# Streaming both parts of x in one 512-column matmul for the feature-form products of a two-layer block in fp32r

## The chip, the cores and the metric

One Trainium2 chip, one of its cores. The metric is the device time of one execution in microseconds. Engines: TensorE (PE) does matmuls, ScalarE (ACT) and VectorE (DVE) elementwise work, GpSimd (POOL) small steps, SyncE (SP) starts the DMAs.

## What is computed

Two transformer-like layers over 256 tokens of width 1024, in float32. Layer one: an mLSTM branch, a gated short convolution and a stick-breaking attention, all fed by one projection of the normalised input, merged by sigmoid gates; then a squared-ReLU MLP:

```python
h = rmsnorm(x, norm_mix_g)
proj = h @ w_in                        # 1024 x 15368, split in 15 parts
merged = (sigmoid(g_ml) * (y_ml @ w_ml_proj) + sigmoid(g_sc) * (y_sc @ w_sc_proj)
          + sigmoid(g_sb) * (y_sb @ w_sb_proj))
x = x + merged @ w_out
h2 = rmsnorm(x, norm_mlp_g)
x = x + square(relu(h2 @ w_up)) @ w_down       # 1024 x 4096, 4096 x 1024
```

Layer two mixes an RG-LRU branch, gated linear attention and block attention from `w_in_2`, projects with `w_out_2`, and has a gated feed-forward part of width 2816 (`w_ffn_gate_2`, `w_ffn_up_2`, `w_ffn_down_2`).

## The kernel before

All weights stream once through SBUF. A product is made of groups of up to 512 output columns; a group's weights come in units of 4 k-tiles (4 x 128 rows) by 512 columns, 1 MB each. `land` has three slots for units; SP loads unit u once `wlo` of unit u-3 is made.

Each float32 operand is split in two fp32r parts. For weights, `split(u)` does it: ACT copies `land` to `whi` (line 865), DVE subtracts to get `wlo` (line 1210); both have three slots, and ACT waits until PE has done unit u-3. For activations the parts are `xT_hi` and `xT_lo` and the like, made when a transposed tile leaves PSUM (`turn_split`). A product is hi x hi + hi x lo + lo x hi: three matmuls.

In `product(u, between)` token-form groups hold 128 tokens stationary and stream up to 512 weight columns (lines 500 to 502). Feature-form groups hold 128 weight columns stationary and stream the 256 tokens of x three times: `whi` against `xT_hi`, `whi` against `xT_lo`, `wlo` against `xT_hi` (lines 508, 510, 512), all into the same 256 columns of PSUM. `acc` has two halves of two banks each, taken by groups in turn: group n waits until group n-2 has been read.

Feature-form are the queries and keys of both attentions, the short convolution's parts (scc, scu, scb), up0 to up7, and in layer two lru, mqk0, mqk1, gqk and gu0 to gu10, a gate and an up part of 256 columns each in one group. The rest is token-form.

The order on each engine is written out by hand. The loops of ACT and DVE run over units u. At u each first does `split(u + 2)`, then the steps listed for that u, among them the eviction if u is the last unit of its group. ACT and DVE work in order, so whatever waits there holds all that stands behind it:

- up: DVE waits for PE, does max(acc, 0) x row from PSUM (line 1669), ACT squares it (1134) and rounds it to `aT_hi` (1137); DVE makes `aT_lo` (1469) in the next iteration, after its `split`.
- gu: DVE multiplies the gate part (1741) and the up part (1743) by the row, ACT takes the sigmoid (1186), DVE multiplies twice (1747, 1748), ACT rounds to `a2T_hi` (1188), DVE makes `a2T_lo` (1476) an iteration later.
- scb: DVE multiplies `conv` (1624), ACT rounds (1128), DVE subtracts (1628); `conv_taps` is twelve small steps (1307, 1309).

Between products PE also does the attention heads and the turns (transposes, line 527). Before up, lru and gu the input is normalised anew: `turn_split` of h2, h3, h4, squares on ACT, a root on POOL, a diagonal on DVE (1225) and a `row`.

Of the kernel before, what the change touches and what calls it, by code (L numbers as in the profile page):

```python
# [5 lines left out]
F32 = mybir.dt.float32  # L6
# [5 lines left out]
P = 128  # L12
# [59 lines left out]

def plan_groups():

    g = []

    def halves(name, weight, col, act, form, k=KD):
        for j in range(2):  # L80
            g.append((f"{name}{j}", weight, [(col + j * NG, NG)], k, act, form))

    halves("sbq", "w_in", C_SBQ, "xT", "feat")
    halves("sbk", "w_in", C_SBK, "xT", "feat")
    halves("sbv", "w_in", C_SBV, "xT", "tok")
    halves("mlq", "w_in", C_MLQ, "xT", "feat")
    halves("mlk", "w_in", C_MLK, "xT", "feat")
    halves("mlv", "w_in", C_MLV, "xT", "tok")
    halves("mlo", "w_in", C_MLO, "xT", "tok")
    halves("scc", "w_in", C_SCC, "xT", "feat")  # L90
    halves("scu", "w_in", C_SCU, "xT", "feat")
    halves("scb", "w_in", C_SCB, "xT", "feat")
    for b, col in (("sb", C_GSB), ("ml", C_GML), ("sc", C_GSC)):
        for j in range(2):
            g.append((f"g{b}{j}", "w_in", [(col + j * NG, NG)], KD, "xT", "tok"))
            g.append((f"p{b}{j}", f"w_{b}_proj", [(j * NG, NG)], KD, f"y{b}T", "tok"))
    halves("out", "w_out", 0, "mT", "tok")
    for j in range(D_FF // NG):
        g.append((f"up{j}", "w_up", [(j * NG, NG)], KD, "xT", "feat"))
# [5 lines left out]
    g.append(("gqk", w2, [(C2_GQ, 2 * P)], KD, "xT", "feat"))
    g.append(("gout", w2, [(C2_GOUT, GLA_H * GLA_DV)], KD, "xT", "tok"))
    g.append(("mv", w2, [(C2_MV, NG)], KD, "xT", "tok"))
    g.append(("mqk1", w2, [(C2_MQ + 2 * P, 2 * P), (C2_MK + 2 * P, 2 * P)], KD, "xT", "feat"))
    halves("mix", "w_out_2", 0, "y2T", "tok")
    for j in range(D_FF2 // GU):  # L110
        g.append((f"gu{j}", ("w_ffn_gate_2", "w_ffn_up_2"), [(j * GU, GU), (j * GU, GU)], KD, "xT", "feat"))
    halves("dn", "w_ffn_down_2", 0, "a2T", "tok", KF2)
    return g


GROUPS = plan_groups()
G_AT = {grp[0]: n for n, grp in enumerate(GROUPS)}
UNITS = [(n, k, min(UK, grp[3] - k)) for n, grp in enumerate(GROUPS) for k in range(0, grp[3], UK)]


_at = UNITS.index((G_AT["mix0"], 0, UK))
UNITS[_at:_at + 4] = [(G_AT[f"mix{j}"], k, m) for k, m in ((0, 4), (4, 2), (6, 2)) for j in range(2)]
# [7 lines left out]
def width(n):  # L130
    return sum(w for _, w in GROUPS[n][2])
# [20 lines left out]
for _name, _k, _ in TURNS:  # L152
# [7 lines left out]
U_IF = 1  # L160
TURN_SB = ML0 + 6
TURN_ML = TURN_SB + 2
B2 = FIRST_U["lru"]

MB_AT = [(B2 + 11, 4), (B2 + 12, 2), (B2 + 12, 4), (B2 + 13, 2), (B2 + 14, 1), (B2 + 14, 3), (B2 + 15, 1),
         (B2 + 15, 2), (B2 + 15, 4), (B2 + 16, 1), (B2 + 16, 2)]
MB_TURN0, MB_TURN1 = (B2 + 15, 3), (B2 + 17, 1)


def build(nc, dram, out):  # L170
# [19 lines left out]
    row = sb("row", [P, T])  # L190
    vecs = sb("vecs", [P, V_ROWS])
# [68 lines left out]
    relu = sb("relu", [P, 2, 2 * NG], stack=ffn)  # L260
    relu2 = sb("relu2", [P, 2, 2 * NG], stack=ffn)
# [55 lines left out]
    half_hi, half_lo = sem("half_hi"), sem("half_lo")  # L317
# [42 lines left out]
    def land_count(u):  # L360

        return 16 * sum(len(GROUPS[UNITS[v][0]][2]) for v in range(u % LANDS, u + 1, LANDS))
# [5 lines left out]
    def _(sp):  # L368
# [17 lines left out]

        for u in range(NU):
# [8 lines left out]
            if u == 5:  # L396
# [5 lines left out]
            if u == FIRST_U["up1"]:  # L402
# [3 lines left out]
            if u == B2 + 4:  # L406
# [29 lines left out]
    def _(pe):  # L436
# [12 lines left out]
        def wait_operand(name, act, k1):  # L449

            if act == "xT":
                turned_ready("h2" if name[:2] == "up" else
                             "h4" if name[:2] == "gu" else
# [7 lines left out]
            elif act == "yscT":  # L461
                pe.wait_ge(ysc_lo, (k1 + 3) // 4)
# [10 lines left out]
        def product(u, between):  # L473
# [12 lines left out]
            if u == 0:  # L486
                pe.wait_ge(half_lo, 1)
# [1405 lines left out]
```

## Time and profile before

| | us |
|---|---|
| median of 3 runs | 964.78 (964.78 to 964.8) |
| span of the profiled execution | 964.4 |
| PE busy | 935.6 (97%) |
| DVE busy | 579.0 (60%) |
| ACT busy | 469.0 (49%) |
| DMA, mean of 16 engines | 170 GB/s |
| mean granted TensorE clock | 0.991 |

The share of busy time counts when an engine has any instruction under way. For PE it includes overlap of one matmul with the next, so the spacing of starts tells more.

### The profile page before, as it was taken

The numbers are of one execution on the slowest core, as the hardware profiler recorded it, in microseconds if no ns is written. First come the engines' busy times: TensorE is split into PE (matmuls) and PEld (weight loads), VectorE is DVE, ScalarE is ACT, GpSimd is POOL, SyncE is SP. The second block draws the span as 40 slices with busy tenths as digits, with TensorE's granted clock in tenths as the row PEclk, the third lists the DMA queues.
The fourth block names the chain that finished last, engine by engine and source line by source line (L and its number), as shares of the span: only waits on it lengthen the run. The fifth ranks groups of instructions, "written<-read, shape, count | busy, mean of one in ns | idle before, by whom it ended". The sixth has DMA issues, their size and how long they took to land.

```text
span 964.4 us, 14152 instructions
## 1 busy us (share of the span) xinstructions
PE 935.6 (97%) x6003; PEld 842.0 (87%) x6003; DVE 579.0 (60%) x610; ACT 469.0 (49%) x520; POOL 38.6 (4%) x75
## 2 busy tenths in 40 slices
PE   5999999999999999999999999998999799999996
PEld 4998998899998888888999988898788699999884
DVE  4554645577787445555556644557975666666552
ACT  6334776862445334344555534446654554444341
POOL 0000111120010000000000000010000000000000
PEclk9999999999999999999999999999999799999999
DMA  8567444443255655555555565528612555556641
GB/s 265 186 234 230 147 161 144 133 150 113 88 175 178 207 184 199 193 175 196 175 175 175 175 218 177 195 77 259 218 67 69 171 176 176 175 176 200 211 135 44
DMA packets 99375, 164.01 MB, mean 170 GB/s; under 512 B 4833, under 2 KB 37316, under 8 KB 99185
## 3 DMA queue, kind: packets, MB, share of 16 engines
q1 hardware_dynamic: 99312, 163.11, 51.9%
q8 instruction: 47, 0.77, 0.3%
q14 instruction: 16, 0.12, 0.0%
HBM read 162.03 MB, written 3.16 MB: 171 GB/s over the span
## 4 chain that ended last, share of the span: by engine, by line
PE 93%; DVE 2%; DMA 2%; ACT 2%; issue 1%; SPq 1%; POOL 0%; DVEq 0%; ACTq 0%; POOLq 0%
PE acc L508 14%; PE acc L500 14%; PE acc L510 14%; PE acc L512 14%; PE acc L502 14%; PE acc L501 14%; DMA land<-in_w_in 2%; PE m L527 1%; PE m L574 1%; PE m L563 1%; PE m L552 1%; DVE wlo L1210 0%; ACT lw L988 0%; DVE x_tok L1486 0%; PE m L636 0%
## 5 line engine op out<-in xcount | busy, mean ns | idle before, releaser
L1210 DVE TENSOR_TENSOR wlo<-land,whi 128x2048 fp32r<-128x2048 f32 (+2 forms) x153 | 337.1, 2206 | 242.1 <-ACT whi L865 240.4
L865 ACT ACTIVATE whi<-land 128x2048 fp32r<-128x2048 f32 (+2 forms) x153 | 281.7, 1846 | 233.4 <-PE acc L502 164.5
L508 PE MATMUL acc<-xT_hi,whi 128*128 128x256 f32 x1168 | 335.3, 287 | 2.1 <-DVE xT_lo L1247 1.8
L510 PE MATMUL acc<-xT_lo,whi 128*128 128x256 f32 x1168 | 332.2, 284 | 0.0
L512 PE MATMUL acc<-xT_hi,wlo 128*128 128x256 f32 x1168 | 332.1, 284 | 0.0
L508 PEld LDWEIGHTS acc<-xT_hi,whi 128*128 128x128 f32 x1168 | 225.8, 193 | 6.8 <-issue 4.2
L510 PEld LDWEIGHTS acc<-xT_lo,whi 128*128 128x128 f32 x1168 | 225.9, 193 | 0.1
L512 PEld LDWEIGHTS acc<-xT_hi,wlo 128*128 128x128 f32 x1168 | 225.8, 193 | 0.0
L500 PE MATMUL acc<-whi,xT_hi 128*128 128x512 f32 (+2 forms) x240 | 91.9, 383 | 0.0
L502 PE MATMUL acc<-whi,xT_lo 128*128 128x512 f32 (+2 forms) x240 | 90.5, 377 | 0.0
L501 PE MATMUL acc<-wlo,xT_hi 128*128 128x512 f32 (+2 forms) x240 | 90.3, 376 | 0.0
L500 PEld LDWEIGHTS acc<-whi,xT_hi 128*128 128x128 f32 x240 | 45.4, 189 | 9.1 <-issue 0.7
L502 PEld LDWEIGHTS acc<-whi,xT_lo 128*128 128x128 f32 x240 | 45.3, 189 | 8.3
L501 PEld LDWEIGHTS acc<-wlo,xT_hi 128*128 128x128 f32 x240 | 45.4, 189 | 7.8
L500 PE MATMUL acc<-whi,aT_hi 128*128 128x512 f32 x128 | 50.6, 396 | 0.0
L501 PE MATMUL acc<-wlo,aT_hi 128*128 128x512 f32 x128 | 50.6, 395 | 0.0
L502 PE MATMUL acc<-whi,aT_lo 128*128 128x512 f32 x128 | 50.6, 395 | 0.0
L501 PE MATMUL acc<-wlo,a2T_hi 128*128 128x512 f32 x88 | 34.8, 395 | 0.0
L502 PE MATMUL acc<-whi,a2T_lo 128*128 128x512 f32 x88 | 34.8, 395 | 0.0
L500 PE MATMUL acc<-whi,a2T_hi 128*128 128x512 f32 x88 | 34.8, 395 | 0.0
L1186 ACT ACTIVATE sig<-act 128x512 f32<-128x512 f32 x11 | 7.0, 633 | 47.4 <-DVE act L1741 47.4
L502 PEld LDWEIGHTS acc<-whi,aT_lo 128*128 128x128 f32 x128 | 24.0, 187 | 5.9
(337 smaller groups left out, 1077.7 us busy)
## 6 DMA issues: line engine op xcount, KB each, us to landing
land<-in_w_in SPq DMA_DIRECT2D x56, 1024.0 KB, 5.1
land<-in_w_up SPq DMA_DIRECT2D x16, 1024.0 KB, 5.3
land<-in_w_down SPq DMA_DIRECT2D x16, 1024.0 KB, 5.1
land<-in_w_ffn_gate SPq DMA_DIRECT2D x22, 512.0 KB, 4.1
land<-in_w_ffn_up SPq DMA_DIRECT2D x22, 512.0 KB, 5.3
land<-in_w_ffn_down SPq DMA_DIRECT2D x10, 1024.0 KB, 5.2
land<-in_w_out SPq DMA_DIRECT2D x6, 1024.0 KB, 5.1
land<-in_w_in SPq DMA_DIRECT2D x12, 512.0 KB, 4.5
```

The lines of the kernel that those rows point to most:

```text
L500: mm(to, xh[:, k0 + k, ts], whi[:, s, k, 0:w], start=first, stop=False)
L501: mm(to, xh[:, k0 + k, ts], wlo[:, s, k, 0:w], start=False, stop=False)
L502: last = mm(to, xl[:, k0 + k, ts], whi[:, s, k, 0:w], start=False, stop=end)
L508: mm(to, whi[:, s, k, cs], xh[:, k0 + k, :], start=first and c % 2 == 0, stop=False, skip_group_check=True)
L510: mm(to, whi[:, s, k, cs], xl[:, k0 + k, :], start=False, stop=False, skip_group_check=True)
L512: last = mm(to, wlo[:, s, k, cs], xh[:, k0 + k, :], start=False, stop=end, skip_group_check=True)
L527: last = nc.tensor.transpose(M[bank + b][:, (i * TT + t) * P:(i * TT + t + 1) * P], src[:, t, col0 + k * P:col0 + (k + 1) * P], ident)
L552: mm(z[:, 0:T], sbkT[o:o + SB_D, c, 0:P], sbqT[o:o + SB_D, c, :], start=True, stop=True)
L563: mm(z[:, 0:3 * P], sums_r[:, 0:P], w, start=False, stop=True, skip_group_check=True)
L574: last = mm(to, a[:, at:at + P], sbv[:, t, v], start=False, stop=True, skip_group_check=True)
L865: activate(whi[:, u % PARTS, 0:m, 0:w], land[:, u % LANDS, 0:m, 0:w], ACT.Copy).then_inc(hi_ready, 1)
L1210: v.tensor_tensor(wlo[:, u % PARTS, 0:m, 0:w], land[:, u % LANDS, 0:m, 0:w], whi[:, u % PARTS, 0:m, 0:w].bitcast(F32), ALU.subtract).then_ ...
```

## The change

Feature-form products stream x's two parts in one matmul. `xT` now holds both parts side by side, `[P, KD, 2, T]`; `whi` against it gives 512 columns into one bank, hi x hi in the first half and hi x lo in the second; `wlo` against `xT_hi` adds 256 columns to the second half. A bank now holds 128 features, so a group has 256 (two banks) and not 512, and a unit of 2048 columns is 8 k-tiles by 256. The two halves are added at eviction: ACT copies the second half to `rest` (`rest_copy`), DVE adds it to the first (`join`). Constant scales move from the eviction into the weight split. sbq0 with sbq1, up0 with up1, lrx with lrg and ga0 with gu0 are woven in units of 4 k-tiles. The gated part has separate groups ga and gu. The scratch of software DMA is set to 8192.

```diff
-        for j in range(2):
-            g.append((f"{name}{j}", weight, [(col + j * NG, NG)], k, act, form))
+    def quarters(name, weight, col, n=4):
+        for j in range(n):
+            g.append((f"{name}{j}", weight, (col + j * FW, FW), KD, "xT", "feat"))
...
+        step = KD if form == "feat" and name not in PAIRED and name != "gqk" else UK
...
+PAIRED = ("sbq0", "sbq1", "up0", "up1", "lrx", "lrg", "ga0", "gu0")
...
                     for c in range(w // P):
-                        to = acc[:, n % 2, c // 2, (c % 2) * T:(c % 2 + 1) * T]
                         cs = slice(c * P, (c + 1) * P)
-                        mm(to, whi[:, s, k, cs], xh[:, k0 + k, :], start=first and c % 2 == 0, stop=False,
-                           skip_group_check=True)
-                        mm(to, whi[:, s, k, cs], xl[:, k0 + k, :], start=False, stop=False,
-                           skip_group_check=True)
-                        last = mm(to, wlo[:, s, k, cs], xh[:, k0 + k, :], start=False, stop=end,
+                        mm(acc[:, n % 2, c, :], wh[:, k, cs], xT[:, k0 + k].rearrange("p i t -> p (i t)"), start=first,
+                           stop=False, skip_group_check=True)
+                        last = mm(acc[:, n % 2, c, T:2 * T], wl[:, k, cs], xh[:, k0 + k, :], start=False, stop=end,
                                   skip_group_check=True)
...
+        def rest_copy(n):
+
+            at = FEATS.index(n)
+            product_done(GROUPS[n][0])
+            if at >= 2:
+                act.wait_ge(read_dve, reads_before(FEATS[at - 2], "dve"))
+            activate(rest[:, at % 2], rest_part(n), ACT.Copy).then_inc(rest_out, 1)
...
+            if ends and name[:3] == "scb" or ends and name[:2] == "up":
+                rest_copy(n)
...
+            if ends and GROUPS[n][5] == "feat" and name[:3] != "scb" and name[:2] != "up":
+                rest_copy(n)
...
+        def join(to, n):
+
+            dve.wait_ge(rest_out, FEATS.index(n) + 1)
+            return v.tensor_tensor(to, main_part(n), rest[:, FEATS.index(n) % 2], ALU.add)
...
-                v.scalar_tensor_tensor(out=relu[:, j % 2, :].rearrange("p (a b) -> p a b", b=T),
-                                       in0=flat.rearrange("p (a b) -> p a b", b=T), scalar=0.0,
-                                       in1=along(4), op0=ALU.max, op1=ALU.mult).then_inc(read_dve, 1)
+                r = relu[:, j % 2, :].rearrange("p (a b) -> p a b", b=T)
+                link(join(r, n))
+                v.scalar_tensor_tensor(out=r, in0=r, scalar=0.0, in1=along(2), op0=ALU.max,
+                                       op1=ALU.mult).then_inc(read_dve, 1)
...
+                a = act2[:, j % 2, :].rearrange("p (a b) -> p a b", b=T)
+                join(a, n).then_inc(read_dve, 1)
+                dve.wait_ge(read_dve, reads_before(n, "dve"))
+                v.tensor_tensor(a, a, along(2), ALU.mult).then_inc(gate2_ready, 1)
+            if ends and name[:2] == "gu":
+                j = int(name[2:])
+                product_done(name)
+                a, b = act2[:, j % 2, :], up2[:, j % 2, :].rearrange("p (a b) -> p a b", b=T)
+                link(join(b, n))
+                v.tensor_tensor(b, b, along(2), ALU.mult).then_inc(read_dve, 1)
```

ACT's steps for ga are `rest_copy`, a wait for `gate2_ready` and the sigmoid; for gu `rest_copy`, a wait for `act2_ready` and the copy to `a2T_hi`. For scb and up `rest_copy` stands right behind `split(u + 2)`, before ACT's wait for DVE. The steps of the second mixer are moved by two units.

## Rows read from the trace of the kernel before

**Rows 1.** The page: busy time of the engines, and the chain that ended last

```profile
PE 935.6 (97%) x6003; PEld 842.0 (87%) x6003; DVE 579.0 (60%) x610; ACT 469.0 (49%) x520; POOL 38.6 (4%) x75
...
PE 93%; DVE 2%; DMA 2%; ACT 2%; issue 1%; SPq 1%; POOL 0%; DVEq 0%; ACTq 0%; POOLq 0%
```

**Rows 2.** Timeline of PE (start, length in us): feature form, then token form

```profile
499.79 0.28 PE L508 MATMUL acc<-xT_hi,whi 128*128 128x256 f32 x1
...
502.91 0.28 PE L512 MATMUL acc<-xT_hi,wlo 128*128 128x256 f32 x1
...
199.78 0.39 PE L500 MATMUL acc<-whi,xT_hi 128*128 128x512 f32 x1
...
201.82 0.39 PE L500 MATMUL acc<-whi,xT_hi 128*128 128x512 f32 x1
```

**Rows 3.** Groups by line and shape: count, busy us, mean ns, idle before, releaser

```profile
L508 PE MATMUL acc<-xT_hi,whi 128*128 128x256 f32 x1168 | 335.3, 287 | 2.1 <-DVE xT_lo L1247 1.8 <-issue 0.3
...
L1210 DVE TENSOR_TENSOR wlo<-land,whi 128x2048 fp32r<-128x2048 f32 x141 | 322.4, 2289 | 229.7 <-ACT whi L865 229.5
L865 ACT ACTIVATE whi<-land 128x2048 fp32r<-128x2048 f32 x141 | 269.2, 1912 | 221.3 <-PE acc L502 156.1 <-PE acc L512 61.1 <-DMA land<-in_w_in 3.8
```

**Rows 4.** Timeline of ACT and DVE in the up stage

```profile
480.63 1.89 ACT L865 ACTIVATE whi<-land 128x2048 fp32r<-128x2048 f32 x1
...
482.56 2.29 DVE L1210 TENSOR_TENSOR wlo<-land,whi 128x2048 fp32r<-128x2048 f32 x1 [4.02 <-ACT whi L865]
484.77 1.22 DVE L1469 TENSOR_TENSOR aT_lo<-relu,aT_hi 128x1024 fp32r<-128x1024 f32 x1
...
488.83 1.23 DVE L1669 SCALAR_TENSOR_TENSOR relu<-acc,row 128x1024 f32<-128x1024 f32 x1 [0.65 <-PE acc L512]
```

**Rows 5.** Timeline of DVE and ACT at one group of the gated stage

```profile
803.27 0.69 DVE L1747 TENSOR_TENSOR act<-act,sig 128x512 f32<-128x512 f32 x1
803.99 0.69 DVE L1748 TENSOR_TENSOR act<-act,up 128x512 f32<-128x512 f32 x1
...
804.72 0.63 ACT L1188 ACTIVATE a2T_hi<-act 128x512 fp32r<-128x512 f32 x1 [1.49 <-DVE act L1748]
805.25 1.90 ACT L865 ACTIVATE whi<-land 128x2048 fp32r<-128x2048 f32 x1
```

**Rows 6.** Timeline of PE: first matmul of up0, of down0, of gu0 and dn0

```profile
452.78 0.28 PE L508 MATMUL acc<-xT_hi,whi 128*128 128x256 f32 x1
...
546.23 0.39 PE L500 MATMUL acc<-whi,aT_hi 128*128 128x512 f32 x1
...
763.04 0.55 PE L508 MATMUL acc<-xT_hi,whi 128*128 128x256 f32 x1 [1.14 <-DVE xT_lo L1247]
...
893.83 0.39 PE L500 MATMUL acc<-whi,a2T_hi 128*128 128x512 f32 x1
```

**Rows 7.** Timeline of DVE: first wlo after the diagonal of h2, h3 and h4

```profile
461.20 4.49 DVE L1210 TENSOR_TENSOR wlo<-land,whi 128x2048 fp32r<-128x2048 f32 x2 [0.32 <-ACT whi L865]
...
647.35 2.48 DVE L1210 TENSOR_TENSOR wlo<-land,whi 128x1088 fp32r<-128x1088 f32 x2
...
774.30 4.49 DVE L1210 TENSOR_TENSOR wlo<-land,whi 128x2048 fp32r<-128x2048 f32 x2 [0.33 <-ACT whi L865]
```

**Rows 8.** Timelines: DVE at the convolution's taps, ACT and PE under the heads

```profile
286.23 1.14 DVE L1307 TENSOR_SCALAR conv<-zT,vecs 128x256 f32<-128x256 f32 x4
287.41 3.38 DVE L1309 SCALAR_TENSOR_TENSOR conv<-zT,vecs,conv 128x256 f32<-128x256 f32 x8
...
115.34 1.90 ACT L865 ACTIVATE whi<-land 128x2048 fp32r<-128x2048 f32 x1
...
114.71 1.45 PE L574 MATMUL m<-sbv,sba 128*128 128x64 f32 x12
```

**Rows 9.** Timeline of PE, then PE busy, granted clock, DMA share, GB/s by stretch

```profile
690.38 1.91 PE L694 MATMUL m<-gv,kl_tok 64*128 64x256 f32 x6 [2.10 <-DVE kl_tok L1361]
...
692.00:694.00 2.00, 2.00 (x5) 0.50 1.05 350
```

More of the change, by code:

```diff
@@ L70, with halves @@
     V_ROWS += _rows
+FW = 2 * P
 def plan_groups():
     g = []
-    def halves(name, weight, col, act, form, k=KD):
+    def halves(name, weight, col, act, k=KD):
         for j in range(2):
-            g.append((f"{name}{j}", weight, [(col + j * NG, NG)], k, act, form))
[L83 to L87, printed above, removed]
@@ L93, in plan_groups @@
+    quarters("sbk", "w_in", C_SBK)
+    halves("sbv", "w_in", C_SBV, "xT")
+    quarters("mlq", "w_in", C_MLQ)
+    quarters("mlk", "w_in", C_MLK)
+    halves("mlv", "w_in", C_MLV, "xT")
+    halves("mlo", "w_in", C_MLO, "xT")
+    quarters("scc", "w_in", C_SCC)
+    quarters("scu", "w_in", C_SCU)
+    quarters("scb", "w_in", C_SCB)
     for b, col in (("sb", C_GSB), ("ml", C_GML), ("sc", C_GSC)):
         for j in range(2):
-            g.append((f"g{b}{j}", "w_in", [(col + j * NG, NG)], KD, "xT", "tok"))
@@ L105, in plan_groups @@
[L105 to L112, printed above, removed]
+            g.append((f"g{b}{j}", "w_in", (col + j * NG, NG), KD, "xT", "tok"))
@@ L113, in plan_groups, with plan_units, weave @@
+    halves("dn", "w_ffn_down_2", 0, "a2T", KF2)
     return g
 GROUPS = plan_groups()
+FEATS = [n for n, grp in enumerate(GROUPS) if grp[5] == "feat"]
 G_AT = {grp[0]: n for n, grp in enumerate(GROUPS)}
-UNITS = [(n, k, min(UK, grp[3] - k)) for n, grp in enumerate(GROUPS) for k in range(0, grp[3], UK)]
-_at = UNITS.index((G_AT["mix0"], 0, UK))
-UNITS[_at:_at + 4] = [(G_AT[f"mix{j}"], k, m) for k, m in ((0, 4), (4, 2), (6, 2)) for j in range(2)]
+def plan_units():
+    u = []
+    for n, (name, _, _, k, _, form) in enumerate(GROUPS):
+        step = KD if form == "feat" and name not in PAIRED and name != "gqk" else UK
+        u += [(n, at, min(step, k - at)) for at in range(0, k, step)]
+    def weave(first, pieces):
+        at = u.index((G_AT[first], 0, UK))
+        u[at:at + 4] = [(G_AT[first] + j, k, m) for k, m in pieces for j in range(2)]
+    for first in PAIRED[::2]:
+        weave(first, ((0, 4), (4, 4)))
+    weave("mix0", ((0, 4), (4, 2), (6, 2)))
+    return u
@@ L130, in width @@
 def width(n):
-    return sum(w for _, w in GROUPS[n][2])
+    return GROUPS[n][2][1]
+SCALED = {"sbq": SB_D ** -0.5, "mlk": ML_D ** -0.5, "mq0": MB_D ** -0.5, "mq1": MB_D ** -0.5}
 def readers(name):
@@ L360, in land_count, with piece, main_part, rest_part @@
     def land_count(u):
-        return 16 * sum(len(GROUPS[UNITS[v][0]][2]) for v in range(u % LANDS, u + 1, LANDS))
+        return 16 * (u // LANDS + 1)
+    def piece(of, slot, u):
+        n, _, m = UNITS[u]
+        return of[:, slot, 0:m * width(n)].rearrange("p (k n) -> p k n", n=width(n))
+    def main_part(n):
+        return acc[:, n % 2, :, 0:T]
+    def rest_part(n):
+        return acc[:, n % 2, :, T:2 * T]
     block = ctx.enter_context(nc.Block())
@@ L401, in _ @@
                 sp.dma_start(by_query, by_distance.to_broadcast([P, MB_H * 2 * T])).then_inc(copies_out, 16)
-            if u == FIRST_U["up1"]:
+            if u == FIRST_U["up2"]:
                 sp.wait_ge(turn_lo, TURN_AT["merged"] + 4)
@@ L1182, in _ @@
                 act.wait_ge(read_act, reads_before(n, "act"))
-            if ends and name[:2] == "gu":
+            if ends and name[:2] == "ga":
                 j = int(name[2:])
@@ L1732, in _ @@
                 residual(6)
-            if ends and name[:2] == "gu":
+            if ends and name[:2] == "ga":
                 j = int(name[2:])
```

299 lines of the change are left out of this document (146 added, 153 removed).

## The prediction

> **What bounds the kernel now.** I read the page's busy line and its chain that ended last first: TensorE is busy for 97% of the span, and 93% of the chain is PE, spread over the six matmul lines of `product` [rows 1]. Such a busy share says little of what a matmul costs, because matmuls overlap; the distance between starts does. In a stretch of feature-form products 26 intervals take 502.91 - 499.79 = 3.12 us, 0.120 us for 256 columns; in a stretch of token-form products 9 intervals take 2.04 us, 0.2267 us for 512 columns [rows 2]. So 256 more columns cost 0.1067 us, and each matmul has 0.0133 us on top. That last part is what fewer, longer matmuls can save.
>
> Next the helpers of a unit: ACT rounds 2048 columns of weights (`whi`, 1.91 us), DVE takes the rest (`wlo`, 2.29 us), and PE uses them two units later [rows 3]. A feature unit of 48 matmuls takes PE 5.76 us. How close ACT and DVE are to that is seen only in the order of their queues. In the up stage (a group is two units, 11.52 us) DVE evicts each group after a wait of only 0.65 us for PE [rows 4]. So PE leads, with little to spare.
>
> **The change: the stream.** For each k-tile and 128 features, three matmuls of 256 columns become one of 512 and one of 256: 0.360 becomes 0.2267 + 0.120 = 0.3467 us, 0.0133 less. There are 1168 such triples [rows 3], so at most 15.5 us. A unit of 16 triples takes 5.55 us. The up stage has 256 triples and the gated stage 352; if those stages are bound by something else, the other 560 give 7.5 us.
>
> One rule speaks against even this. The trace shows 0.0133 us per matmul [rows 2]. The Trainium skill, "TensorE: Matmul & The Clock Gate", section "Back-to-back issue gap", gives about 2.5 ns beyond the columns for an isolated matmul at the fast clock; by that the 1168 matmuls removed would give an estimated 2.9 us. I take the row.
>
> **The up stage.** The eviction is now ACT's copy of one bank half, DVE's `join`, a second DVE step, then ACT's square and copy, all for each group of 256, which is now a single unit. Follow the two in-order queues. ACT at unit u: `split(u+2)`, `rest_copy`, then a wait for DVE's eviction of u, square, copy. DVE at unit u: `split(u+2)`, which waits for ACT's; `relu_rest` of the group before; `join`; the relu step. ACT's next `split` stands behind its wait, so the work is one ring that goes round once per unit:
> - ACT `whi` 1.89 + 0.04 to DVE's start = 1.93; DVE `wlo` 2.21 from start to start [rows 4].
> - `relu_rest` at 512 columns: 0.69 long, less the 0.08 by which neighbours that don't wait overlap: 0.61; `join` with its own wait 0.72 from start to start, as a multiply of 128x512; relu step 0.69 + 0.04 = 0.73 [rows 5].
> - ACT square 0.63 + 0.04 = 0.67, copy 0.53 from start to start [rows 5]. `rest_copy`, 0.63, runs under `wlo` and is free.
>
> Sum 7.40 us against 5.55 of PE. In the kernel before, `wlo` of every second unit lay off this ring, and 11.52 us of PE covered two units.
>
> The opening: in rows 7 `wlo` follows the statistics of h2 and starts at 461.20, 8.4 us into the stage. The turn now comes 1.4 us earlier, so it starts 7.0 in and, being half size, ends at 8.2. But the four woven half units want it at 6.4 (two of 2.78 us and a turn of 0.8): 1.8 us idle. From there `wlo` of up2 ends at 11.6, the row copy, one turn of the ring for each of up0 and up1, and the split for unit 6 of the stage is done 26.3 us in. Unit 18, down0's first, has its split 12 turns later: 26.3 + 12 x 7.40 = 115.1, and its bank is free 0.61 + 0.72 + 0.73 later: 117.2 us. Before, the stage took 546.23 - 452.78 = 93.45 [rows 6]. Cost +23.7 us.
>
> **The gated stage.** The same ring, in pairs. Gate unit: 1.93 + 2.21 + act2_rest 0.61 + join 0.72 + multiply 0.73 + sigmoid 0.53 = 6.73. Up unit: 1.93 + 2.21 + join, multiply, multiply 3 x 0.72 + multiply 0.73 + copy 0.53 = 7.56. A pair 14.29 against 11.10 of PE. The opening (h4's turn, squares and diagonal, whose `wlo` starts at 774.30 [rows 7], some 2.5 us sooner with the earlier turn) puts the split of unit 6 about 27.0 in; nine pairs are 128.6, and the first dn0 unit starts 1.3 later: 156.9. Before: 893.83 - 763.04 = 130.8 [rows 6]. Cost +26.1 us.
>
> **Smaller places.** All groups get one more DVE step of 0.72 or so and an ACT copy of 0.63; where ACT waits for no eviction this lies beside 5.55 us of PE and costs nothing; uncovered it would be 1.35 us a group.
> - h3's opening: the statistics end as before, `wlo` of the third unit starts no sooner than 647.35 [rows 7], and ends at 648.6. With two half units and a turn PE wants it at 644.6: 4 us idle. A low clock after it is some 1.5 more: with the rest, +6. The chains of the second mixer behind it get `join` steps on queues that stalled PE for 2.10 us before [rows 9]: between 0 and +6 for the extra, I take +2, nearest to two evictions. Together +8.
> - scb, where ACT also waits: `wlo` 2.21, join, multiply 1.44, ACT copy 0.67, rest 0.69, and six tap steps, half of the 1.14 + 3.4 us of rows 8, make 7.3 us for one unit. With the turns of ysb and yml in between I follow the queues to idle of 2.2 + 1.3 + 0.8 = 4.3 us before psb0. Bounds 0 and 7.
> - heads over mlq and mlk: ACT takes its next `whi` at 115.34, 0.63 us after PE's unit ended at 114.71 [rows 8]; a 0.63 copy ahead of it makes `sbw_lo` come 0.3 to 0.4 late for `sb_remain`, four times: +1.5. Bounds 0 and 4.
> - start: half of the first weights is split before the turn; the 16 transposes bind soon after: -0.5. The scaling that moves into the splits keeps their length; mq, mk and mlq get no cheaper. The DMA bytes are the same, and 5 us of landing lie inside three units. `rest` and the smaller scratch are memory only.
>
> **The sum.** -7.5 + 23.7 + 26.1 + 8.0 + 4.3 + 1.5 - 0.5 = +55.6 on a span of 964.4: 1020.0, and with the 0.4 us that the profiled execution's span lies below the median of 964.8, 1020.4 us.
>
> **Rivals.** *The queues are no ring.* If eviction stayed hidden, the stream's 15.5 us would come out: about 949 us. For it: ACT and DVE are busy for only 49% and 60% [rows 1]. Against it: both queues are in order and the waits stand in the code; busy shares don't see a ring. 6%.
>
> *The clock makes it worse.* PE now idles 1.6 to 1.9 us in each unit. After an idle of 2.10 us ahead of the start at 690.38 the granted clock read 0.50 from 692 to 694 us, that is 1.2 GHz [rows 9]. At 1.2 GHz a unit takes 16 x (0.427 + 0.213) = 10.2 us, and with half of the work there 7.9. That is 0.5 over the ring in 14 up units and 0.75 in 20 gated ones: +22, so 1042; it decides once over 40% of the work runs slow. Against it: a slow spell of some 3 us after each gap costs 1.5 us and still fits into 7.40, and without a gap the clock comes back. The Trainium skill (same page, "A second HAM failure mode: psum-queue depth-cycling") tells of such swinging between the two rates from short idles between groups. 12%.
>
> *The slower side with a smaller bill.* The openings and the small places cost nothing, only the rings: about 1005. 12%, inside the range.
>
> *The 512-column matmul doesn't save its fixed part*: 7.5 us more, 1028. 4%.
>
> **How the numbers follow.** The forecast has 64%, the rivals what stands with them, 2% is left for terms that happen to cancel. The low end is 1005 less 0.15 us in each of 34 ring units, 1000; the high end takes in the clock at half, 1044. Faster than 0.2%: 0.06; within 0.2%, about what a measurement of this kernel can tell from no change: 0.02; slower 0.92.
>
> **What would show it.** Right: feature matmuls alternate 0.227 and 0.120 us; in up and gated stages ACT's `whi` starts 7.4 and 7.15 us apart on average with no wait for PE before it, PE idles once a unit on `wlo` or the bank's release, and down0 starts 117 us after up0; token stages as before. Wrong: `whi` still waits for PE there (then 949), or unit times above 7.9 at a clock below 1 (then 1042 and more).

## The result and the profile after

The changed kernel takes 1028.2 us (1027.25 to 1030.25, 4 runs) against 964.79 (964.78 to 964.91): 1.0663 times as long, 95% interval 1.0647 to 1.0679. The forecast was 1020.4 in a range of 1000 to 1044. The profiled execution has a span of 1026.1 us.

First the page of the changed kernel: busy time of each engine, and the chain that ended last by engine.

```profile
PE 937.2 (91%) x4835; PEld 777.1 (76%) x4835; DVE 620.8 (60%) x702; ACT 507.2 (49%) x618; POOL 38.4 (4%) x75
...
PE 61%; DVE 16%; ACT 11%; issue 10%; DMA 1%; POOL 1%; DVEq 0%; SPq 0%; ACTq 0%; POOLq 0%
```

PE's share fell from 97% to 91% and its part of the chain from 93% to 61% [rows 1]: DVE, ACT and `issue` (time in which an engine waited for nothing that the profile shows) now hold 37% of the chain. ACT is busy for 49% and DVE for 60%, as before. An engine can be on the critical path for a tenth of the span without its busy share moving.

Where the time went is read from the starts of the first matmul of each stage:

| stage | before, us | after, us | difference | forecast |
|---|---|---|---|---|
| start to up0 | 452.78 | 451.83 | -0.95 | -0.7 |
| up0 to down0 (up stage) | 93.45 | 117.15 | +23.7 | +23.7 |
| down stage | 90.46 | 92.23 | +1.8 | 0 |
| lru to gu0/ga0 (second mixer) | 126.35 | 134.41 | +8.1 | +6.5 |
| gated stage | 130.79 | 158.41 | +27.6 | +26.1 |
| dn0 to the end | 70.6 | 72.1 | +1.5 | 0 |

The forecasts of the first and the fourth row contain the stream's saving there (448 and 112 triples at 0.0133 us). The timeline of PE of the changed kernel has the bounds of the two slow stages:

```profile
451.83 0.39 PE L545 MATMUL acc<-xT,whi 128*128 128x512 f32 x1
...
568.98 0.51 PE L538 MATMUL acc<-whi,aT_hi 128*128 128x512 f32 x1 [1.57 <-DVE relu L1718]
...
795.62 0.76 PE L545 MATMUL acc<-xT,whi 128*128 128x512 f32 x1 [1.10 <-DVE xT L1302]
...
954.03 0.50 PE L538 MATMUL acc<-whi,a2T_hi 128*128 128x512 f32 x1 [1.61 <-DVE act L1266]
```

One turn of the ring, in the timelines of ACT and of DVE (start, length in us, line, and in brackets the idle time before it and who ended it):

```profile
474.11 1.90 ACT L898 ACTIVATE whi<-land 128x2048 fp32r<-128x2048 f32 x1
475.91 0.57 ACT L940 ACTIVATE rest<-acc 128x512 f32<-128x512 f32 x1
480.30 0.63 ACT L1176 ACTIVATE relu<-relu 128x512 f32<-128x512 f32 x1 [3.81 <-DVE relu L1718]
480.96 0.63 ACT L1179 ACTIVATE aT_hi<-relu 128x512 fp32r<-128x512 f32 x1
481.50 1.90 ACT L898 ACTIVATE whi<-land 128x2048 fp32r<-128x2048 f32 x1
```

```profile
476.04 2.29 DVE L1258 TENSOR_TENSOR wlo<-land,whi 128x2048 fp32r<-128x2048 f32 x1 [3.17 <-ACT whi L898]
478.25 0.68 DVE L1524 TENSOR_TENSOR aT_lo<-relu,aT_hi 128x512 fp32r<-128x512 f32 x1
478.85 0.68 DVE L1266 TENSOR_TENSOR relu<-acc,rest 128x512 f32<-128x512 f32 x1
479.57 0.69 DVE L1718 SCALAR_TENSOR_TENSOR relu<-relu,row 128x512 f32<-128x512 f32 x1
```

From `whi` at 474.11 to the next at 481.50 are 7.39 us. Follow who waits: ACT idles 3.81 us for DVE's relu step, DVE 3.17 us for ACT's `whi`, and nobody for PE. In the kernel before, `whi` was held up by feature-form matmuls for 61.1 us in all and DVE's eviction by PE [rows 3, 4]. Here ACT is idle for half of a turn and DVE for 43% of it, at different times, and yet the turn has no slack: while one of them works on its steps of the ring, the other has nothing that it may start.

The waits of the changed kernel, grouped (us in total, times, longest), with the granted clock of a stretch in each slow stage behind them (PE, PEld, DVE, ACT and POOL busy, PEclk, DMA share, GB/s):

```profile
ACT relu L1176 <- DVE relu L1718: 58.7, 16, 3.8
ACT a2T_hi L1234 <- DVE act L1800: 52.0, 11, 4.7
...
ACT sig L1230 <- DVE act L1790: 38.3, 11, 3.8
...
PE acc L545 <- DVE relu L1718: 19.3, 13, 1.6
...
PE acc L545 <- DVE act L1266: 14.8, 9, 1.7
```

```profile
460.00:565.00 105.00, 85.70 (x471) 71.60 (x471) 59.61 (x58) 51.08 (x58) 0.00 (x0) 1.00 0.50 160
805.00:945.00 140.00, 117.06 (x642) 97.76 (x643) 89.97 (x88) 58.90 (x60) 0.00 (x0) 1.00 0.51 162
```

PE waits once per unit, for the step of DVE that gives a bank back: 1.47 to 1.57 us in the up stage, and in the gated stage by turns 1.60 to 1.70 us ahead of a gate unit or the down stage and 0.93 to 1.03 us ahead of an up unit. The clock is 1.00 in both stretches. Last, the stream itself, from PE's timeline inside one unit:

```profile
475.15 0.40 PE L545 MATMUL acc<-xT,whi 128*128 128x512 f32 x1
...
477.98 0.40 PE L545 MATMUL acc<-xT,whi 128*128 128x512 f32 x1
```

Eight pairs take 2.83 us, 0.3537 each. The forecast said 0.3467, from 0.2267 + 0.120 [rows 2].

### The profile page after: what moved, and what is told of

Its sections match the earlier page's. It is cut to its first block, busy times and chain, and to the rows that moved or that the text cites. A ratio compares the mean times of both kernels' runs of the same rounds, so it can differ in the third digit from the quotient of the medians.

```text
span 1026.1 us, 12159 instructions
## 1 busy us (share of the span) xinstructions
PE 937.2 (91%) x4835; PEld 777.1 (76%) x4835; DVE 620.8 (60%) x702; ACT 507.2 (49%) x618; POOL 38.4 (4%) x75
## 4 chain that ended last, share of the span: by engine, by line
PE 61%; DVE 16%; ACT 11%; issue 10%; DMA 1%; POOL 1%; DVEq 0%; SPq 0%; ACTq 0%; POOLq 0%
PE acc L538 13%; PE acc L540 12%; PE acc L539 12%; PE acc L545 11%; ACT whi L898 7%; PE acc L547 5%; DVE wlo L1258 3%; DVE relu L1718 1%; PE m L562 1%; ACT rest L940 1%; PE m L609 1%; DVE aT_lo L1524 1%; ACT relu L1176 1%; DVE relu L1266 1%; DVE up L1796 1%
## 5 line engine op out<-in xcount | busy, mean ns | idle before, releaser
L545 PE MATMUL acc<-xT,whi 128*128 128x512 f32 x1168 | 423.6, 405 | 50.0 <-DVE relu L1718 19.3
L547 PE MATMUL acc<-xT,wlo 128*128 128x256 f32 x1168 | 328.5, 281 | 0.0
L545 PEld LDWEIGHTS acc<-xT,whi 128*128 128x128 f32 x1168 | 221.1, 189 | 116.2 <-DVE relu L1718 23.4
L547 PEld LDWEIGHTS acc<-xT,wlo 128*128 128x128 f32 x1168 | 222.3, 190 | 0.1
L538 PE MATMUL acc<-whi,xT 128*128 128x512 f32 (+2 forms) x240 | 92.3, 385 | 2.7 <-DVE conv L1672 1.7
L540 PE MATMUL acc<-whi,xT 128*128 128x512 f32 (+2 forms) x240 | 90.5, 377 | 0.0
L539 PE MATMUL acc<-wlo,xT 128*128 128x512 f32 (+2 forms) x240 | 90.5, 377 | 0.0
L940 ACT ACTIVATE rest<-acc 128x512 f32<-128x512 f32 x73 | 42.7, 585 | 58.1 <-PE acc L547 51.9
L538 PEld LDWEIGHTS acc<-whi,xT 128*128 128x128 f32 x240 | 45.4, 189 | 12.6 <-DVE conv L1672 2.0
L540 PEld LDWEIGHTS acc<-whi,xT 128*128 128x128 f32 x240 | 45.4, 189 | 8.5
L539 PEld LDWEIGHTS acc<-wlo,xT 128*128 128x128 f32 x240 | 45.5, 189 | 7.7
L538 PEld LDWEIGHTS acc<-whi,aT_hi 128*128 128x128 f32 x128 | 24.0, 187 | 9.4 <-DVE relu L1718 1.9
```

The source lines that it names most:

```text
L538: mm(to, xh[:, k0 + k, ts], wh[:, k, :], start=first, stop=False)
L539: mm(to, xh[:, k0 + k, ts], wl[:, k, :], start=False, stop=False)
L540: last = mm(to, xl[:, k0 + k, ts], wh[:, k, :], start=False, stop=end)
L545: mm(acc[:, n % 2, c, :], wh[:, k, cs], xT[:, k0 + k].rearrange("p i t -> p (i t)"), start=first, stop=False, skip_group_check=True)
L547: last = mm(acc[:, n % 2, c, T:2 * T], wl[:, k, cs], xh[:, k0 + k, :], start=False, stop=end, skip_group_check=True)
L940: activate(rest[:, at % 2], rest_part(n), ACT.Copy).then_inc(rest_out, 1)
```

## Experiments

The theory: the up and gated stages are paced by a ring of ACT and DVE that goes round once per unit of 16 triples, 7.4 us against 5.6 of PE, because ACT's next `whi` stands behind its wait for DVE's eviction. If it is right, the new matmuls and their eviction can stay as they are, and only the next `split` has to be issued ahead of that wait. Rivals: the two DVE steps and the ACT copy that were added are simply too much work; PE itself is slower; the clock. The kernel before gave 965.48 us beside e1 to e4, 965.31 beside e5 to e8, 965.58 beside e9 and e10 and 963.68 beside e11; ratios are to these.

**e1, the ring opened in the up stage.** ACT issues `split(u + 3)` right behind `rest_copy(n)`, DVE right behind the relu step, and the next iteration leaves it out.

```diff
+EARLY = {LAST_U[_g[0]] for _g in GROUPS if _g[0][:2] in ('up',)}
-            if u != LAST_U["mix1"]:
+            if u != LAST_U["mix1"] and u - 1 not in EARLY:
                 split(u + 2)
...
                 rest_copy(n)
+                if u in EARLY:
+                    split(u + 3)
...
                                        op1=ALU.mult).then_inc(read_dve, 1)
+                if u in EARLY:
+                    split(u + 3)
```

> The changed kernel, with one order changed in the up stage alone: ACT makes whi of unit u+3 right behind rest_copy of unit u, before it waits for DVE's eviction, and DVE makes wlo of u+3 right behind the relu step; no instruction is added or removed. Ring theory: the ring of 7.39 us per unit is cut, PE (5.55 us a unit) binds again. The up stage falls from 117.2 to about 92 us, the wait of down0's third unit (1.4 us) goes, the gated stage stays at 158 us: about 1001 us. Rival (DVE and ACT have simply more work per unit): the same work in another order, the up stage stays within 3 us of 117, about 1028 us. Rival (the clock or the matmul form): also 1028.

Measured: 1002.06 us (1.0373, interval 1.0307 to 1.0439). The up stage takes 93.32 us instead of 117.15, with every operation still in it; the gated stage stays at 158.38. Timeline of ACT of this kernel:

```profile
482.06 0.60 ACT L941 ACTIVATE rest<-acc 128x512 f32<-128x512 f32 x1 [1.72 <-PE acc L548]
482.56 1.91 ACT L899 ACTIVATE whi<-land 128x2048 fp32r<-128x2048 f32 x1
484.37 0.62 ACT L1179 ACTIVATE relu<-relu 128x512 f32<-128x512 f32 x1
485.01 0.63 ACT L1182 ACTIVATE aT_hi<-relu 128x512 fp32r<-128x512 f32 x1
487.71 0.60 ACT L941 ACTIVATE rest<-acc 128x512 f32<-128x512 f32 x1 [2.06 <-PE acc L548]
```

The square stands behind `whi` and waits for nobody; ACT waits for PE instead, 2.06 us. A turn is 5.65 us. So what paced the up stage was the order of the two queues, not the amount of work in them.

**e2, the ring made longer.** The changed kernel with the square of the up stage done twice.

```diff
+                link(activate(relu2[:, j % 2, :], relu[:, j % 2, :], ACT.Square))
```

> The changed kernel with ACT's square in the up stage done twice (the first result is overwritten by an equal one). Ring theory: each of the 14 or 15 turns of the ring that precede down0 gets longer by 0.63 + 0.04 = 0.67 us, though ACT is busy for only half of the time: the ring goes from 7.39 to 8.06 us, the up stage from 117.2 to about 126.8, the time to about 1038 us. Rival (ACT has slack, the excess sits elsewhere): no change, 1028 us.

Measured: 1041.78 us (1.0784, interval 1.0716 to 1.0852), the up stage 126.41. A step of 0.67 us in the ring costs 0.66 per turn, though ACT sits idle for nearly half of it. The time is 3.8 us above the 1038 expected: outside the ring, the second mixer took 138.8 us instead of 134.4, with a mean granted clock of 0.92 from 671 to 810 us against 0.97 in the changed kernel's second mixer. This kernel also shows what the clock does to the ring. PE's timeline at three turns, then two stretches of 2 us, one behind the first and one behind the third of these starts, with the granted clock in the third column from the end:

```profile
497.12 0.49 PE L545 MATMUL acc<-xT,whi 128*128 128x512 f32 x1 [2.13 <-DVE relu L1719]
...
505.16 0.51 PE L545 MATMUL acc<-xT,whi 128*128 128x512 f32 x1 [0.62 <-DVE relu L1719]
...
513.22 0.49 PE L545 MATMUL acc<-xT,whi 128*128 128x512 f32 x1 [2.13 <-DVE relu L1719]
```

```profile
500.00:502.00 2.00, 2.00 (x8) 1.71 (x8) 1.12 (x1) 1.34 (x2) 0.00 (x0) 0.50 0.06 21
...
514.00:516.00 2.00, 2.00 (x14) 1.74 (x13) 0.00 (x0) 1.97 (x3) 0.00 (x0) 1.00 0.93 328
```

After the idle of 2.13 us ahead of 497.12 the clock goes to 0.50 (1.2 GHz) for some 3 us, so this unit ends later and the idle behind it is only 0.62 us. The unit from 505.16 runs at 1.00, and the idle behind it is 2.13 again; but this time the clock stays at 1.00 through the next unit, and falls only behind the following idle, 2.24 us ahead of 521.27. In the whole stage five of eight idles of 2.13 to 2.24 us were followed by 0.50: the first two slow spells are two turns apart, the later ones three. They cost nothing here, since the starts stay 8.05 us apart with or without a slow spell: it is taken out of the idle behind it.

**e3, both rings opened.** As e1, with `EARLY` for ga and gu too: ACT behind `rest_copy(n)`, DVE behind ga's multiply and gu's last one.

```diff
-EARLY = {LAST_U[_g[0]] for _g in GROUPS if _g[0][:2] in ('up',)}
+EARLY = {LAST_U[_g[0]] for _g in GROUPS if _g[0][:2] in ('up', 'ga', 'gu')}
```

> The order change of the up stage made in the gated stage too (ga and gu units). Ring theory: both stages are bound by PE. Up stage about 92, gated stage 158.4 to about 128 us, the two waits of 1.4 to 1.7 us in the first units of down0 and dn0 gone: what stays of the difference from the kernel before is -1.0 before up, -1.6 and -2.7 in the two stages, +9.8 between down0 and ga0 and about +1.3 outside the span: about 970 us. Rival (more work on ACT and DVE): about 1028. If the stream's saving were not real, these two stages would come out 3.4 and 4.7 us longer: 978.

Measured: 970.07 us (1.0038, interval 1.0015 to 1.0060); up stage 93.27, gated stage 128.99, 1.8 below the kernel before. Of the 61.7 us by which the span had grown 55.6 are gone (1026.1 to 970.5), and nothing was taken out.

**e4, e3 with three matmuls again.** Everything as in e3, but the 512-column matmul done as two of 256: the stream alone undone.

```diff
-                        mm(acc[:, n % 2, c, :], wh[:, k, cs], xT[:, k0 + k].rearrange("p i t -> p (i t)"), start=first,
+                        mm(acc[:, n % 2, c, 0:T], wh[:, k, cs], xT[:, k0 + k, 0, :], start=first,
                            stop=False, skip_group_check=True)
+                        mm(acc[:, n % 2, c, T:2 * T], wh[:, k, cs], xT[:, k0 + k, 1, :], start=False,
+                           stop=False, skip_group_check=True)
```

> As e3, but the 512-column matmul is issued as two of 256 columns into the same two bank halves (whi with xT_hi, whi with xT_lo): three matmuls again, all else the same. Theory that each matmul has about 0.0133 us on top of its columns: 1168 more of them add 15.5 us to e3, about 985 us, with starts 0.120 us apart. By the Trainium skill (TensorE: Matmul & The Clock Gate, section Back-to-back issue gap) the part beyond the columns is 2.5 ns: an estimated 2.9 us more, 973.

Measured: 979.5 us (1.0143, interval 1.0099 to 1.0188); the spans of the profiled executions differ by 7.7 us. That is 0.0066 us per triple over 1168 triples, half of the 0.0133 of the forecast. The Trainium skill ("TensorE: Matmul & The Clock Gate", "Back-to-back issue gap") gives N / 2.4 + 2.5 ns for an isolated matmul of N columns at the full clock, so 2.5 ns for each matmul removed, an estimated 2.9 us in all. The measured 7.7 us lie between the two and decide. The medians (979.5 against 970.07) are 9.4 us apart; the distance of starts is the cleaner measure. PE's timelines, e4 and then e3:

```profile
499.72 0.28 PE L548 MATMUL acc<-xT,whi 128*128 128x256 f32 x1
...
502.96 0.28 PE L548 MATMUL acc<-xT,whi 128*128 128x256 f32 x1
```

```profile
499.80 0.40 PE L546 MATMUL acc<-xT,whi 128*128 128x512 f32 x1
...
502.98 0.40 PE L546 MATMUL acc<-xT,whi 128*128 128x512 f32 x1
```

Nine triples (27 starts) take 3.24 us, 0.360 each, as forecast; nine pairs (18 starts) take 3.18, 0.3533 each.

**e5, the changed kernel with lrx and lrg not woven.** The third unit of h3's stage is wanted later then.

```diff
-PAIRED = ("sbq0", "sbq1", "up0", "up1", "lrx", "lrg", "ga0", "gu0")
+PAIRED = ("sbq0", "sbq1", "up0", "up1", "ga0", "gu0")
...
-B3 = B2 + 2
+B3 = B2
...
-            if (u, k) == (B3 + 1, 2):
+            if (u, k) == (B3 + 1, 4):
```

> The changed kernel with lrx and lrg not woven: two units of 8 k-tiles in place of four half units, and the row's matmul of h3 at k-tile 4 of the second. Theory of the openings: the third unit's split is tied to the statistics of h3, not to PE; four half units bring the third one 5.6 us sooner to PE than whole ones do. Whole units take away the 3.8 us wait there and add at most 0.5: the stretch from down0 to ga0 falls from 226.6 by 4 to 5 us, the time to about 1023.5 us. Rival (that stretch is longer because of the join steps in the chains of the second mixer): 1028, with the wait merely moved behind.

Measured: 1023.26 us (1.0608, interval 1.0582 to 1.0635), the lru products 14.12 us instead of 19.54. PE's timeline of the changed kernel at that place, then its granted clock:

```profile
673.06 0.51 PE L545 MATMUL acc<-xT,whi 128*128 128x512 f32 x1 [3.78 <-DVE wlo L1258]
```

```profile
674.00:676.00 2.00, 2.00 (x8) 1.70 (x7) 1.34 (x2) 0.00 (x0) 0.00 (x0) 0.50 0.90 254
676.00:678.00 2.00, 2.00 (x9) 1.67 (x8) 0.00 (x0) 0.28 (x1) 0.00 (x0) 0.65 0.85 238
```

The idle of 3.78 us and the slow clock after it are both gone in e5. The same kernel shows that the length of an idle doesn't tell by itself whether the clock falls; PE's timeline of e5, then its granted clock:

```profile
715.71 0.70 PE L729 MATMUL m<-gv,kl_tok 64*128 64x256 f32 x4 [2.74 <-DVE kl_tok L1416]
```

```profile
716.00:718.00 2.00, 2.00 (x11) 1.43 (x10) 2.00 (x2) 0.73 (x2) 0.00 (x0) 1.00 0.85 306
```

The clock stays at 1.00 behind this idle of 2.74 us, where the kernel before fell to 0.50 behind one of 2.10 at the same step [rows 9].

**e6, e3 and e5 together.**

> e3 and e5 together: the splits of up, ga and gu ahead of ACT's waits, lrx and lrg as whole units. If ring and opening are independent, their gains add: 970 - 4.5 = about 965.5 us, level with the kernel before. If the wait was only moved, 970.

Measured: 963.54 us (0.9990, interval 0.9975 to 1.0005): the kernel before, within what can be told. It is 2 us less than expected, with executions from 961.1 to 967.4. The up stage takes 92.03 us here against 93.27 in e3, with the same matmuls in the same order. PE's timeline:

```profile
499.69 0.39 PE L546 MATMUL acc<-xT,whi 128*128 128x512 f32 x1
...
502.81 0.40 PE L546 MATMUL acc<-xT,whi 128*128 128x512 f32 x1
```

Nine pairs take 3.12 us, 0.3467 each: the forecast's value. In this execution two long stretches run so (from 28.6 to about 62 us and from 470 to 542 us), while the gated stage of the same execution has 0.3536 a pair, and the same stretches have 0.3534 to 0.3539 in the profiled executions of e1, e3 and e7.

**e7, e6 with the early split for the scb units too** (DVE's behind the scb step of the same unit, ACT's behind `rest_copy`).

```diff
-EARLY = {LAST_U[_g[0]] for _g in GROUPS if _g[0][:2] in ('up', 'ga', 'gu')}
+EARLY = {LAST_U[_g[0]] for _g in GROUPS if _g[0][:2] in ('up', 'ga', 'gu') or _g[0][:3] == 'scb'}
...
                 v.tensor_tensor(y, b, y, ALU.mult).then_inc(read_dve, 1)
+                if u in EARLY:
+                    split(u + 3)
```

> e6 with the same order of splits in the four scb units, where ACT also waits for DVE's eviction. Ring theory: the three waits in the first units behind scb (1.7, 1.1 and 0.4 us) go, as far as DVE's own work (taps, turns of ysb and yml, the row scaling) leaves room: 2 to 3.5 us less than e6, about 962.5 us. Rival (DVE is simply full there): as e6, 965.5.

Measured: 962.37 us (0.9965, interval 0.9947 to 0.9982). Behind scb PE now waits 0.54 us where the changed kernel waited 1.69, 1.06 and 0.44. In the time the step is smaller than the 2 to 3.5 us expected: 1.2 us less than e6, and the two intervals overlap, so it is the trace and not the time that shows the gain. This version is faster than the kernel before by 0.2 to 0.5%, and by the two ratios it takes 6.5% less than the changed one. The stream is worth 7.7 us in the comparison of e4 with e3; about 3 are left. The kernel before with early splits of its own was not run.

**e8, the kernel before with the scratch of software DMA set to 8192,** a part of the change that is no instruction. It was to explain why the times of the changed kernel lie 1.7 us above their spans, when the forecast had 0.4 for the kernel before.

```diff
-    nc = bacc.Bacc("TRN2", target_bir_lowering=False, num_devices=1)
+    nc = bacc.Bacc("TRN2", target_bir_lowering=False, num_devices=1, dynamic_dma_scratch_size=8192)
```

> The kernel before with the software DMA scratch at 8192, as the changed kernel has it, and nothing else. The changed kernel's runs lie 1.7 us above their spans, those of the kernel before 0.4. If the scratch setting makes that, 1.3 us more than before, at the same span; if not, no change.

Measured: 964.32 us (0.9994, interval 0.9981 to 1.0007), no change. The 29 executions of the kernel before beside it themselves lie 1.7 to 2.2 us above their spans (964.71 against 962.9, for one). The 0.4 set a median of 964.8 against the span of one profiled execution, whose own time is not on record; it is no property of the kernel.

**e9, e7 with 512 columns in both matmuls.** `wlo` too meets both parts of x, which adds the product lo x lo that the other kernels drop.

```diff
-                        last = mm(acc[:, n % 2, c, T:2 * T], wl[:, k, cs], xh[:, k0 + k, :], start=False, stop=end,
+                        last = mm(acc[:, n % 2, c, :], wl[:, k, cs], xT[:, k0 + k].rearrange("p i t -> p (i t)"), start=False, stop=end,
```

> The kernel of e7 (both products in order, rings opened), where the 256-column matmul of each triple is widened to 512 columns: wlo too is multiplied with both parts of x, so that the product lo x lo, which was dropped, is added in as well. 1168 matmuls have 256 more columns. It asks what the 0.353 us between the starts of two pairs consist of. Theory A, the 512-column matmul of the feature form takes what the token form's takes, 0.2267 us, and the 0.0067 us beyond 0.3467 come from mixing the two widths: pairs start 0.453 us apart, which is +0.10 x 1168 = +117 us where PE sets the pace, a unit 7.25 us. Theory B, every 512-column matmul of the feature form takes 0.0067 more than the token form's: pairs 0.467 apart, +133 us, a unit 7.47 us. From 962 us: about 1079 by A, 1095 by B. The distance of starts is what tells them apart, since units this long may hide other waits.

Measured: 1071.9 us (1.1101, interval 1.1052 to 1.1151), 7 us below theory A. In the profiled executions the second mixer, bound by other waits too, grew by only 4.4 us over e7 where its 112 triples would give 11.2. What the question hangs on is the distance of starts. Its PE timeline:

```profile
520.24 0.39 PE L546 MATMUL acc<-xT,whi 128*128 128x512 f32 x1
520.47 0.39 PE L548 MATMUL acc<-xT,wlo 128*128 128x512 f32 x1
...
528.86 0.39 PE L546 MATMUL acc<-xT,whi 128*128 128x512 f32 x1
```

38 intervals take 8.62 us, 0.2268 each: the token form's value. So a 512-column matmul of the feature form costs what it should among its like, a 256-column one too (e4), and the missing 0.0067 us per pair appear only where the two widths take turns, in most such stretches but not in all (e6). Why, no run here shows.

**e10, the kernel before with its square doubled.** Does the kernel before have such a ring, with a slack of 0.65 us?

```diff
+                link(activate(relu2[:, j % 2, :], relu[:, j % 2, :], ACT.Square))
```

> The kernel before, with ACT's square of each group in the up stages done twice (the second writes the same values; the output stays the same). It adds 1.06 + 0.04 = 1.10 us to ACT between DVE's relu step and ACT's next whi. The kernel before has a ring too: whi, wlo, rest and the eviction of 1024 columns go round once per group of two units, 11.52 us of PE, with a slack of 0.65 us, DVE's wait for PE. Theory: the ring takes 10.87 + 1.10 = 11.97 us, 0.45 over PE's 11.52; in the eight groups of the up stage behind the opening that is +3 to +3.6 us, and the stage goes from 93.45 to about 97 us; DVE's evictions stop waiting for PE. Rival: the slack is larger than DVE's wait shows, and the stage stays within 0.5 us of 93.45.

Measured: 964.26 us (0.9983, interval 0.9969 to 0.9997), and the up stage takes 93.45 us, exactly as before. The expectation had the turn nearly right (11.97) and the cost wrong (+3 to +3.6 us). Timeline of DVE, two evictions and the split of down0's unit; then PE's at down0:

```profile
490.03 1.22 DVE L1670 SCALAR_TENSOR_TENSOR relu<-acc,row 128x1024 f32<-128x1024 f32 x1
...
501.90 1.22 DVE L1670 SCALAR_TENSOR_TENSOR relu<-acc,row 128x1024 f32<-128x1024 f32 x1
...
543.85 2.29 DVE L1211 TENSOR_TENSOR wlo<-land,whi 128x2048 fp32r<-128x2048 f32 x1 [5.11 <-ACT whi L865]
```

```profile
546.36 0.39 PE L500 MATMUL acc<-whi,aT_hi 128*128 128x512 f32 x1
```

The ring does take 11.87 us, 0.35 more than PE's 11.52, and the evictions don't wait for PE any more. But the splits run up to two units ahead, and the seven turns eat 2.5 us of that lead. `wlo` for down0 ends at 546.14; PE wants it at 546.36.

**e11, the same with two extra squares**, to see the lead run out.

```diff
+                link(activate(relu2[:, j % 2, :], relu[:, j % 2, :], ACT.Square))
+                link(activate(relu2[:, j % 2, :], relu[:, j % 2, :], ACT.Square))
```

> The kernel before with the square done three times instead of once (two extra, same values). With one extra square (e10) DVE's eviction came every 11.87 us instead of 11.52 and never waited for PE, yet the up stage kept its 93.45 us: the third unit's wlo of each turn fell back by 0.35 us per group, from a lead, and the last one (down0's) ended at 546.14, just ahead of 546.36 where PE wanted it. Theory, a ring slower than PE first eats the lead of the splits, and costs time only from there on: the turn is 11.87 + 1.09 = 12.96, evictions 466.3 + 7 x 12.96 = 557.0, down0's wlo ends 3.26 us before that, at 553.75, so down0 starts at 553.8 instead of 546.36: the up stage takes 100.9 us, +7.4, and the third unit of the down stage waits 0.35 + 1.09 = 1.4 us instead of 0.35. Together +8.8 over the kernel before. Rival, ACT's extra work lies beside PE's whatever its length (PE waits only when engines are busy all the time; ACT would be busy some 75% here): the stage stays within 1 us of 93.45.

Measured: 975.02 us (1.0114, interval 1.0076 to 1.0152), which is 7 to 15 us more, and the +8.8 expected lies in it. The up stage takes 100.98 us (100.9 expected), and the third unit of the down stage waits 1.49 us. PE and DVE at down0:

```profile
552.01 0.47 PE L500 MATMUL acc<-whi,aT_hi 128*128 128x512 f32 x1 [1.22 <-issue]
```

```profile
549.62 2.29 DVE L1212 TENSOR_TENSOR wlo<-land,whi 128x2048 fp32r<-128x2048 f32 x1 [6.20 <-ACT whi L865]
```

The split for down0 ends at 551.91, and PE starts with it (this stage began 1.9 us earlier than in e10). PE waits 1.22 or 1.23 us ahead of five starts that are 12.97 us apart, down0's the last of them: once the lead is gone, each turn costs all that the ring is longer than PE's 11.52 us. One extra square costs nothing and two cost 7.5 us in this stage.

## Why the prediction was right, and where it was off

**The ring: right.** The steps were read from rows 4 and 5 one by one, 7.40 us; the trace shows 7.39, and the up stage's +23.7 is met. So is the opening on which it stands: the split of the stage's unit 6 ends 26.5 us in (476.04 + 2.29, less 451.83), where 26.3 was forecast. e1 shows that it is the ring (same work, 23.8 us less), e2 that each of its steps counts in full. The rival "the queues are no ring" falls.

**The gated stage: +27.6 instead of +26.1.** A pair of units takes 14.37 us, not 14.29 (903.39 to 917.76 between PE's starts): 0.7 in nine pairs. The opening took 0.8 longer than the 28.3 us put down for it. e3 takes the whole back.

**The stream: right in kind, half in size.** This is the term of the sum that failed. The step "0.2267 + 0.120" added two distances of starts, each read from a stream of one width. Side by side they take 0.3533 to 0.3537. The term of -7.5 outside the rings was about -3.8: +3.7 us on the sum, spread over the first and fourth rows of the table. e4 gives the size, e9 that it comes with the alternation. It isn't fixed: two stretches of e6 run at the forecast's 0.3467, so what sets the spacing stays open.

**Two waits that were not followed: +1.8 and +1.5.** The sum took the token stages "as before", at nothing: the step "down0 starts 117.2 us in" stopped at down0. PE's timeline of the changed kernel shows the stage's third unit late, behind both rings:

```profile
581.83 0.50 PE L538 MATMUL acc<-whi,aT_hi 128*128 128x512 f32 x1 [1.39 <-DVE wlo L1258]
...
967.21 0.50 PE L538 MATMUL acc<-whi,a2T_hi 128*128 128x512 f32 x1 [1.70 <-DVE wlo L1258]
```

The third unit of each token stage has its split behind the last eviction of the ring. In e3 both stages are back to the length before or just below it (90.46 and 70.0 us). e11 shows the same wait in the kernel before once its ring is too long.

**h3's opening: right.** Forecast 4 us idle and 1.5 of low clock, +6; measured 3.78 idle, the clock at 0.50 and 0.65 from 674 to 678, and the lru products 6.7 longer. e5 takes 5.4 of it away. The rest of the second mixer is +1.3 us where +2 was taken, less the stream's share; it is made of +0.9, -2.3, +1.3, -0.2 and +1.7 by stretch between changes of form. PE's waits account for most of it. In the timeline of PE of the kernel before, then of the changed one:

```profile
664.58 0.38 PE L665 MATMUL m<-con,gv 128*16 128x128 f32 x2 [2.12 <-ACT lw L988]
```

```profile
687.78 0.43 PE L758 MATMUL m<-lw,wab 64*64 64x256 f32 x2 [0.84 <-DVE lw L1477]
...
721.42 0.49 PE L729 MATMUL m<-gv,kl_tok 64*128 64x256 f32 x2 [2.74 <-DVE kl_tok L1416]
...
757.26 0.37 PE L670 MATMUL m<-mbqk 64*128 64x128 f32 x1 [1.88 <-DVE mbqk L1750]
```

The wait of 2.12 us is gone and one of 0.84 stands a stretch earlier, the wait for `kl_tok` grew from 2.10 [rows 9] to 2.74, and the one of 1.88 for `mbqk` is new. So the +2 was near the sum of terms that partly cancel, which the forecast didn't name.

**scb and the heads.** Waits of 1.69 + 1.06 + 0.44 = 3.2 us stand where 2.2 + 1.3 + 0.8 were forecast; with the small ones between, the stretch is 3.8 longer than the stream alone would leave it. e7 removes most. The heads' +1.5 didn't come: the ml stage is 0.7 shorter, about the stream's 0.9 (128 triples at 0.0067). The start gave -1.0 instead of -0.5, and the sb stage behind it is 1.7 shorter, 0.8 more than the stream explains; that was not traced.

**The clock rival: it didn't come in either ring.** It was to decide at idles of 1.6 to 1.9 us in each unit. The idles were 1.47 to 1.57 in the up stage and by turns 0.93 to 1.03 and 1.60 to 1.70 in the gated stage, and the clock read 1.00 throughout both rings. The Trainium skill (same page, "A second HAM failure mode: psum-queue depth-cycling") describes swinging between the two rates from short idles between groups. The rings of the changed kernel don't show it; e2's ring does, with idles of 2.13 to 2.24 us. There the forecast's argument against the rival holds, that a spell of some 3 us fits into the turn: it cost nothing. Its assumption that each gap brings a slow spell doesn't: five of eight did.

**Outside the span: 1.3 us** of the forecast's miss, since 0.4 was taken and 1.7 came. The kernel before has 1.7 to 2.2 beside e8 too, so the change is not its cause.

Sum: the missed 6.1 us of span are 3.3 at the third units, 1.5 in the gated stage, 1.6 in the second mixer and -0.3 ahead of up0, where the smaller saving of the stream (+3.0) and the terms that cost less than forecast cancel. With the 1.3 outside the span and the 0.4 by which the profiled execution lies below the median, that is the 7.8 us between 1020.4 and 1028.2. That the row ahead of up0 comes so close is luck, since it is a sum of misses of opposite sign.

## What to carry to other kernels

Two in-order engines that hand work to and fro form a ring; write down its steps once from the timeline and compare its length with the bound engine's time for the same unit, because busy shares (49% and 60% here) don't show it. Halving the group, with the unit of weights as large as before, puts an eviction into every unit and not into every second one, beside a weight split that stays as long. The cure here was not less work but issuing the next unit's split ahead of the wait (55.6 us of span, without removing an instruction). A ring that is slightly too long first eats the lead of its buffers (e10, no cost) and then costs its excess in every turn (e11), and its tail reaches the third unit of the next stage, the first whose split is issued behind the ring's last eviction.

## What the runs showed of the hardware

- Matmuls of one width with weights of their own start 0.120 us (256 columns) and 0.2267 us (512) apart; taking turns, a pair takes 0.3533 to 0.3537 us in the stretches shown of the changed kernel and e3, and the sum, 0.3467, in one of e6.
- Idles of 1.47 to 1.57 us in every 7.39 (up stage), and of 0.93 to 1.03 and 1.60 to 1.70 by turns (gated stage), left the granted clock at 1.00.
- Idles of 2.10 [rows 9] and 3.78 us were followed by 0.50. So were five of eight of 2.13 to 2.24 us in e2's up stage; the other three, one of 2.12 in the kernel before (at 664.58) and one of 2.74 in e5 (at 715.71) were not.
- In e2 the slow spells of some 3 us, two or three turns apart, cost nothing, since they were taken out of the following idle.
